# The order of the 24 products in a dense block: high part of the weights first, low part last

## The reference, cut to what matters

```python
h = rms_norm(x, norm_mix_pre[l])
z = h @ w_in[l]
...
kv = mem_n @ w_xkv
...
f = jnp.square(jax.nn.relu(h @ w_ff1[l])) @ w_ff2[l]
x = x + rms_norm(f, norm_ff_post[l])
...
proj = h @ w_in
```

## Time and profile before

| | us |
|---|---|
| median of 3 runs | 2458.14 |
| lowest and highest run | 2456.86, 2459.35 |
| the profiled execution's own time | 2457.28 |
| its span, first to last instruction | 2455.6 |
| TensorE products busy | 2263.6 (92%) |
| VectorE busy | 995.2 (41%) |
| ScalarE busy | 1014.3 (41%) |
| GpSimd busy | 832.7 (34%) |
| mean granted TensorE clock | 0.96 |

### The profile page before, as it was taken

One profiled execution on the slowest core, in us unless ns is written; L12 is line 12 of the kernel. 1 busy time (PEld: TensorE's weight loads), 2 busy tenths in 40 slices (PEclk: granted clock), 3 DMA queues, 4 the chain that ended last, 5 costly groups with the idle time before them and its releaser, 6 DMA issues.

```text
span 2455.6 us, 32458 instructions
## 1 busy us (share of the span) xinstructions
PE 2263.6 (92%) x11652; PEld 1863.2 (76%) x11652; DVE 995.2 (41%) x1858; ACT 1014.3 (41%) x1911; POOL 832.7 (34%) x404
## 2 busy tenths in 40 slices
PE   7988988799998886999998889999999889999998
PEld 5776766687888775888887777777777677777776
DVE  4788888434413113323221443222352523222361
ACT  5766665724234332333222333444542423444631
POOL 2422222144444312344443333333343333333342
PEclk9999999899998997999999799999999899999999
DMA  3211111123333201233332322222232322222231
GB/s 134 78 61 47 60 56 47 61 94 95 95 95 103 69 27 43 77 98 99 94 95 68 99 77 70 77 64 75 69 95 70 116 78 69 69 69 69 78 92 54
DMA packets 51744, 189.46 MB, mean 77 GB/s; under 512 B 6564, under 2 KB 7204, under 8 KB 51108
## 3 DMA queue, kind: packets, MB, share of 16 engines
q1 hardware_dynamic: 48096, 175.13, 23.6%
q10 hardware_dynamic: 2452, 6.88, 0.8%
q0 software_dynamic: 1072, 5.77, 0.6%
HBM read 185.66 MB, written 2.10 MB: 76 GB/s over the span
## 4 chain that ended last, share of the span: by engine, by line
PE 70%; DVE 14%; issue 5%; ACT 4%; DVEq 4%; POOL 1%; POOLq 0%; DMA 0%; ACTq 0%
PE bank L334 19%; PE bank L335 18%; PE bank L336 18%; PE bank L406 3%; PE bank L845 2%; PE bank L888 2%; POOL weight_lo L369 1%; PE bank L871 1%; ACT weight_hi L364 1%; DVE attention_work L1575 1%; ACT wide_region L969 1%; DVE wide_region L1937 1%; DVE work_region L1599 1%; DVEq L1541 1%; DVE wide_region L1940 1%
## 5 line engine op out<-in xcount | busy, mean ns | idle before, releaser
L369 POOL TENSOR_TENSOR weight_lo<-weight_slots,weight_hi 128x1024 fp32r<-128x1024 f32 x286 | 690.6, 2415 | 1171.8 <-ACT weight_hi L364 1171.8
L364 ACT ACTIVATE weight_hi<-weight_slots 128x1024 fp32r<-128x1024 f32 x286 | 302.5, 1059 | 887.3 <-PE bank L336 815.5
L334 PE MATMUL bank<-h_hi,weight_hi 128*128 128x512 f32 x1248 | 509.0, 408 | 38.2 <-DVE h_lo L386 19.2
L335 PE MATMUL bank<-h_lo,weight_hi 128*128 128x512 f32 x1248 | 493.9, 396 | 0.0
L336 PE MATMUL bank<-h_hi,weight_lo 128*128 128x512 f32 x1248 | 493.2, 395 | 0.0
L334 PEld LDWEIGHTS bank<-h_hi,weight_hi 128*128 128x128 f32 x1248 | 238.6, 191 | 93.7 <-issue 26.1
L336 PEld LDWEIGHTS bank<-h_hi,weight_lo 128*128 128x128 f32 x1248 | 238.7, 191 | 51.9
L335 PEld LDWEIGHTS bank<-h_lo,weight_hi 128*128 128x128 f32 x1248 | 239.1, 192 | 44.8
L369 POOL TENSOR_TENSOR head_weight_lo<-weight_slots,head_weight_hi 128x1024 fp32r<-128x1024 f32 x42 | 104.1, 2481 | 293.1 <-ACT head_weight_hi L364 293.1
L334 PE MATMUL bank<-h_hi,head_weight_hi 128*128 128x512 f32 x336 | 139.4, 415 | 5.4 <-DVE h_lo L386 2.9
L335 PE MATMUL bank<-h_lo,head_weight_hi 128*128 128x512 f32 x336 | 132.9, 395 | 0.0
(11 more groups left out here) (433 smaller groups left out, 4274.5 us busy)
## 6 DMA issues: line engine op xcount, KB each, us to landing
weight_slots<-weights SPq DMA_DIRECT2D x328, 512.0 KB, 3.6
wide_region<-cmp_w ACTq DMA_DIRECT2D x2, 2048.0 KB, 8.4
v_region<-ssm_bc POOLq DMA_DIRECT2D x8, 256.0 KB, 4.7
residual<-x_in POOLq DMA_DIRECT2D x1, 2048.0 KB, 9.2
out<-normed SPq DMA_DIRECT2D x4, 512.0 KB, 2.6
residual<-x_in SPq DMA_DIRECT2D x2, 512.0 KB, 5.1
residual<-x_in ACTq DMA_DIRECT2D x2, 512.0 KB, 10.0
v_region<-mem_in POOLq DMA_DIRECT2D x1, 1024.0 KB, 5.3
```

Of the source, the lines that this page charges most:

```text
L334: pe.matmul(to, w_h[:, k, :], hi[:, k, 0:width], start=(k == 0), stop=False)
L335: pe.matmul(to, w_h[:, k, :], lo[:, k, 0:width], start=False, stop=False)
L364: act.activation(parts[0][s % 2], slot[s], ACT.Copy).then_inc(w_hi[s], 1)
L369: eng.tensor_tensor(parts[1][s % 2], slot[s], parts[0][s % 2].bitcast(F32), ALU.subtract).then_inc(w_lo[s], 1)
```

## The change

Within `gemm` the wait for the low part of the weights moves from the head of the block to behind its 16 products with the high part, and the eight products with the low part come after it. At the head the block waits for the high part alone.

```diff
             if part[0] == 0:
-                pe.wait_ge(w_lo[s], quad + 1)
+                pe.wait_ge(w_hi[s], quad + 1)
                 bank_free(pe, quad, s)
             to = bank[s % 2][:, 0:width]
             w_h, w_l = parts[0][s % 2], parts[1][s % 2]
...
                     pe.wait_ge(lo_ready, stage + (k + 1))
                 pe.matmul(to, w_h[:, k, :], hi[:, k, 0:width], start=(k == 0), stop=False)
                 pe.matmul(to, w_h[:, k, :], lo[:, k, 0:width], start=False, stop=False)
+            if part[0] == 0:
+                pe.wait_ge(w_lo[s], quad + 1)
+            for k in part:
                 mm = pe.matmul(to, w_l[:, k, :], hi[:, k, 0:width], start=False, stop=(k == KT - 1))
             if part[-1] == KT - 1:
                 mm.then_inc(mm_done[s], 1)
```

## The result

| | before | after |
|---|---|---|
| median of 22 runs each, us | 2458.94 | 2462.97 |
| lowest and highest run | 2456.52, 2464.46 | 2458.94, 2467.15 |
| the profiled execution's own time | 2457.28 | 2464.11 |
| its span | 2455.6 | 2462.5 |
| mean granted TensorE clock in it | 0.960 | 0.956 |

The ratio is 1.0015, its 95% interval 1.0008 to 1.0021: slower by 3.7 us (2.0 to 5.2), against a forecast of 2465.0, 7.7 us above the profiled execution of before. The interval lies mostly under the 0.2% that the prediction called a change that can be told.

What follows compares the result with a forecast made beforehand. It took TensorE, busy for 92% of the span, to bound the kernel. Waits removed -9.0, order +10.3 and clock +6.4 gave +7.7 us on the profiled 2457.28, so 2465.0; range 2455.5 to 2474.

Steps and rivals of the forecast that it cites:

- the case that had 0.28: Rival for the paced blocks: the clock doesn't mind the gaps, so +1.3 us, 2459, no change; chance 0.28.
- The low end of the range, 2455.5: Whole kernel: low end meant to take in the no-change case and the bounds of the first sum.
- Only eight waits are worth anything, and the steady state pays nothing: Whole span: low weights awaited eight times, 12.6 us in all; feed-forward products stay at 0.227 us, never awaiting them.
- a met wait is free: New wait behind product 16: costs nothing when met; the rival of 0.1 us per block, 31 us, had chance 0.03.
- 476.8: -0.8: Block at 476.78 starts 2.4 us earlier, but the small sums behind await ACT's squares; saves 0.8 us, bounds 0 and 1.6.
- 561.0 and 584.3: -3.6: Two blocks at 560.99 and 584.29: whole waits for low weights go, 2.17 and 1.41 us.
- Memory stage: -4.6: Blocks of 256 columns: five waits for low weights go, 3.8 us plus 5 x 0.16, and nothing is added.
- rival that the small sums get the high clock: 64 sums behind the memory stage keep the high clock, saving 6.0 us at most: 2451.8, faster; chance 0.09.
- The order: 1.42 per start, 1.4 in MG, 1.6 in ACC: Paced blocks: eight low products lie behind the last pair; four starts 5.7, MG 1.4, two ACC 3.2, together +10.3 us.
- The clock: +6.4: Paced blocks: gaps keep TensorE's clock low, 1.2 us in each of four starts (4.8) plus 1.6 in ACC.

Runs made afterwards that it cites:

- 5.: The kernel before with one more, always met wait for the weights' high part before the fifth pair of each whole block; 2458.91 us, ratio 0.9997.
- experiments 4: The changed kernel plus one filler product for each of the first six pieces in four starts and twelve in each ACC start; 2461.25 us, ratio 1.0003.
- 6: The changed kernel, but paced blocks make both high-part products of each piece, then the low-part product of the piece before; 2442.65 us, repeated 2441.85.

## Why the prediction came out as it did

The direction held and the forecast time, 2465.0, is 2 us from the measured 2463.0. Part of this closeness is luck: the change itself was forecast as +7.7 us and measured as +3.7, half of it, and the median of before had meanwhile come out 1.7 us above the profiled execution that the forecast started from. Of the chances, 0.63 lay on slower by over 0.2%; the measured 0.15% is under that line, in the case that had 0.28. The low end of the range, 2455.5, isn't what its parts give: 2457.28 - 9.8 + 10.3 - 1.6 is 2456.2. Step by step:

- *Only eight waits are worth anything, and the steady state pays nothing.* Right: 986 products in 223 us, no wait for `weight_lo` left, a met wait is free (5.).
- *476.8: -0.8.* Wrong in sign, +0.3 to +0.6 in every kernel that has the new order there. The mechanism was named (sums that are capped by the squares, and start with an idle stretch behind them), the second half priced too low: some 23 of them lost the high clock.
- *561.0 and 584.3: -3.6.* Measured -3.3. The second wait is worth its 1.4; the first gave 1.8 instead of 2.17, since that block now waits for ACT, which empties its bank:

```profile
563.85 0.47 PE L334 MATMUL bank<-gelu_hi,weight_hi 128*128 128x512 f32 x1 [0.23 <-ACT attention_work L1129]
```

- *Memory stage: -4.6.* Measured -7.0, the largest error. The waits themselves gave 4.8. The rest the sum had no term for: blocks behind a wait had a first product 0.1 us longer, 0.6 in all with one shorter gap; the sums and the idle time before them took 0.85 less, and the block behind the sums, also a narrow one, 0.7 (5.04 to 4.32), both by the clock. The timeline after has `755.95 12.18` for the 64 sums where the earlier trace rows have 13.02. The rival that the small sums get the high clock came true only by this much; by the windows of after the clock is at 0.50 from 757.71 on, 1.8 us behind their start, where the 0.53 of the earlier trace rows means 0.8 us at the high one:

```profile
757.71:761.01 3.30, 3.30 (x18) 3.30 (x17) 0.00 (x0) 1.72 (x4) 0.00 (x0) 0.50 0.53 164
761.01:767.80 6.79, 6.79 (x34) 6.79 (x33) 0.00 (x0) 0.00 (x0) 0.00 (x0) 0.50 0.00 0
```

- *The order: 1.42 per start, 1.4 in MG, 1.6 in ACC.* Right: 1.43 to 1.45 where the clock is held, 1.5, and 1.64. What the sum had no term for are 1.1 us less between HX's first block and H of layer 0. No wait takes them up: 0.9 of them are the clock in the first block of the feed-forward, at 982.10 in the trace of before, which runs its first 5.28 us at the low level there and 3.41 us in the changed kernel. Windows of before, then of after:

```profile
982.10:987.38 5.28, 5.28 (x13) 4.11 (x14) 0.00 (x0) 0.00 (x0) 0.00 (x0) 0.50 0.00 0
```

```profile
979.56:982.97 3.41, 3.41 (x8) 2.73 (x9) 0.00 (x0) 0.00 (x0) 0.00 (x0) 0.50 0.00 0
```

  The seven traces whose HX block is not as before all have this 0.9; the four others with an old HX have 0.0 to 0.4. Why the clock rises earlier there is open.
- *The clock: +6.4.* Mechanism right, size too large. In the starts 2.9 and 3.6 us instead of 4.8. In ACC of layer 0, where I had put no more of it than before had, order and clock together cost 1.3 and 1.2 us instead of 1.6: the low stretch now lies wholly in this block and no longer reaches into the next. In layer 1 it is 2.6 and 4.2 us instead of 3.2, of which 1.6 falls away against an execution of before in which the clock fell there too. All in all the clock in the paced blocks cost 5.1 and 4.2 us in the two traces of the changed kernel, where the sum has 6.4.

So the memory stage (2.4 us more gain), the clock in the starts (1 to 2 less loss) and the 1.1 us behind HX pull towards a faster kernel, 476.8 (1.1 to 1.4) towards a slower one; they take 7.7 down to 3 or 4. By the rows that the change touches, the two traces of the changed kernel sum to +4.4 and +3.3 us; the medians say +3.7 and +2.0. Had the clock in the paced blocks cost nothing, the gains (-9.8) and the order (+10.5, less 1.1) would nearly have cancelled.

## What to carry to other kernels

When operands arrive piece by piece, count what is left to do behind the last piece: one product in the best version here, three before, ten in the changed one. Work whose operands are there belongs into the gaps, first for its own time and second because here it kept TensorE's clock up (experiments 4 and 6). A change that moves a wait can be right in one class of blocks and wrong in another; price each class, and give each its own order.

## What the runs showed of the hardware that I had not expected

- The clock fell while TensorE was busy without a gap, in the 128x1 sums: in the kernel with only the wide blocks new, 9.90 of 9.90 us busy at 0.50, with 48 of them; in the earlier trace rows the 64 also run without a gap, 39 at 1.00 and the rest at the low clock. Being busy with these small products didn't hold it.
- In ACC the idle time in front of the seventh piece went with the clock behind it: after 3.4 us it fell in eight of eight blocks, after 2.07 us in eight of ten, after 0.7 us (two blocks) and 1.68 us (four) in none.
- Executions of one kernel differ by up to 12 us, and the clock goes with it: of 25 of before in one set the shortest took 2456.4 at 0.960, the longest 2468.1 at 0.955. With 22 runs on each side the interval was 1.6 us to either side, with 11 runs against 29 some 2.5. Two traces laid over each other block by block showed differences of 1 us in single stretches.
